# Moving the latent projection's weight splits and first units into the normalisation before it, and its rotary part to GpSimd

## The reference

```python
def _shared_latent(x, pos, wkv_a, kv_norm):
    kv = x @ wkv_a                      # 1024 -> 256 + 64
    ckv = _rms_norm(kv[..., :KV_LORA], kv_norm)
    kpe = _rope(kv[..., KV_LORA:], pos)
    return ckv, kpe
# and in _mla_query: _rms_norm(x @ wq_a, q_norm), 1024 -> 384
```

## Time and profile before

| | |
|---|---|
| median of three runs | 2543.57 us (2538.87 to 2545.26) |
| profiled execution | 2539.54 us, span 2537.5 us |
| TensorE busy | 2392.3 us, 94% of the span |
| VectorE / ScalarE / GpSimd busy | 51% / 30% / 13% |
| chain that ended last, by engine | PE 82%, DVE 10%, ACT 3%, issue 3%, DMA 1% |
| mean granted TensorE clock | 0.979 |

### The profile page before, as it was taken

How to read it: one execution, slowest core, us unless ns; L and a number is a source line. 1 busy time by engine, 2 the same in 40 slices (tenths; PEclk the granted TensorE clock), 3 DMA queues, 4 the chain that set the end, 5 groups by cost and what they waited for, 6 DMA issues and landing times.

```text
span 2537.5 us, 35304 instructions
## 1 busy us (share of the span) xinstructions
PE 2392.3 (94%) x14022; PEld 2178.8 (86%) x14022; DVE 1287.9 (51%) x2435; ACT 768.2 (30%) x1469; POOL 330.6 (13%) x300
## 2 busy tenths in 40 slices
PE   7899999999999968999998889799999999999997
PEld 7799999999999868898987677587998989999996
DVE  4733343333334675677767787635243443333336
ACT  2331111111111333555546566413311111111112
POOL 2400000000000410000006545033000000000006
PEclk9999999999999989999999999799999999999998
DMA  4121111111111031000005444321211110111111
GB/s 162 42 67 34 50 50 30 36 50 50 50 50 63 13 114 43 19 19 1 12 22 157 155 156 156 133 79 34 67 44 41 50 44 25 50 50 50 51 42 67
DMA packets 137073, 153.84 MB, mean 61 GB/s; under 512 B 10256, under 2 KB 114224, under 8 KB 136808
## 3 DMA queue, kind: packets, MB, share of 16 engines
q1 hardware_dynamic: 124656, 110.07, 13.9%
q0 software_dynamic: 12288, 41.95, 5.3%
HBM read 142.24 MB, written 10.32 MB: 60 GB/s over the span
## 4 chain that ended last, share of the span: by engine, by line
PE 82%; DVE 10%; ACT 3%; issue 3%; DMA 1%; POOL 0%; SPq 0%; ACTq 0%; DVEq 0%
PE ps L216 23%; PE ps L218 23%; PE ps L217 23%; DVE split L209 4%; PE ps L2136 2%; PE ps L2101 2%; ACT split L204 2%; PE ps L2116 1%; PE ps L2117 1%; PE ps L224 1%; PE ps L223 1%; PE ps L1646 1%; PE ps L2123 1%; DVE plain L292 1%; DVE plain L1889 1%
## 5 line engine op out<-in xcount | busy, mean ns | idle before, releaser
L216 PE MATMUL ps<-split 128*128 128x512 f32 (+6 forms) x3632 | 1236.8, 341 | 56.9 <-DVE split L209 31.9
L217 PE MATMUL ps<-split 128*128 128x512 f32 (+6 forms) x3632 | 1222.8, 337 | 0.0
L218 PE MATMUL ps<-split 128*128 128x512 f32 (+6 forms) x3632 | 1222.3, 337 | 0.0
L216 PEld LDWEIGHTS ps<-split 128*128 128x128 f32 x3632 | 689.6, 190 | 102.6 <-DVE split L209 37.0
L217 PEld LDWEIGHTS ps<-split 128*128 128x128 f32 x3632 | 689.8, 190 | 38.3 <-issue 1.5
L218 PEld LDWEIGHTS ps<-split 128*128 128x128 f32 x3632 | 689.9, 190 | 37.3
L204 ACT ACTIVATE split<-plain 128x1024 fp32r<-128x1024 f32 (+8 forms) x446 | 313.6, 738 | 594.8 <-PE ps L224 365.5
L209 DVE TENSOR_TENSOR split<-plain,split 128x1024 fp32r<-128x1024 f32 (+7 forms) x422 | 362.9, 884 | 190.3 <-ACT split L204 187.1
L998 DVE TENSOR_TENSOR plain<-plain,ps 128x350 f32<-128x350 f32 (+1 forms) x132 | 68.0, 515 | 552.9 <-ACT plain L952 552.3
L276 DVE TENSOR_TENSOR plain<-plain,ps 128x512 f32<-128x512 f32 x360 | 245.0, 685 | 197.0 <-PE ps L218 192.2
L209 DVE TENSOR_TENSOR split<-ps,split 128x512 fp32r<-128x512 f32 (+5 forms) x480 | 247.1, 554 | 136.6 <-ACT split L204 134.6
(11 more groups left out here) (147 smaller groups left out, 1432.1 us busy)
## 6 DMA issues: line engine op xcount, KB each, us to landing
plain<-w_gate SPq DMA_DIRECT2D x44, 512.0 KB, 4.6
plain<-w_up SPq DMA_DIRECT2D x44, 512.0 KB, 4.0
plain<-w_down SPq DMA_DIRECT2D x44, 512.0 KB, 4.4
plain<-x_prompt SPq DMA_DIRECT2D x8, 512.0 KB, 11.2
x_spill<-plain SPq DMA_DIRECT2D x1, 4096.0 KB, 13.9
plain<-wo SPq DMA_DIRECT2D x8, 512.0 KB, 5.3
plain<-x_spill SPq DMA_DIRECT2D x8, 512.0 KB, 7.2
y_prompt<-plain SPq DMA_DIRECT2D x8, 512.0 KB
```

Of the source, the lines that this page charges most:

```text
L216: pe.matmul(out, still[0], moving[0], start=start, stop=False)
L217: pe.matmul(out, still[0], moving[1], start=False, stop=False)
L218: return pe.matmul(out, still[1], moving[0], start=False, stop=stop)
```

## The change

Each block gets places of its own, so that blocks can be split at other times: block 0 in step 3 of the normalisation, 1, 2 and 3 in steps 5, 6 and 7, block 4 in step 11, blocks 5, 6 and the first half of 7 in the first three steps of the latent part, the second half of 7 (which overlies a kv block) when unit 8 is done. Each block is split in two instructions for its two chunks of 128 rows on either engine, and TensorE's units 0 and 9 wait chunk by chunk. Unit 0 moves before the transposes of tile 6, units 1 and 2 before those of tile 7, unit 3 before the tail's; the transposes of the latent rows stand behind unit u + 4 instead of u + 3. VectorE takes units 0 and 1 in step 11 (`behind`). The rotary part goes from VectorE to GpSimd with a semaphore of its own. ScalarE's squares go into PSUM bank 7, so it no longer waits for the output slot; VectorE's scale and GpSimd's rotary part wait for it instead. The diff, cut:

```diff
-def dve_norm_stage(dve, k, ph, nt, turn, scaled, unit0=0, extra=None):
+def dve_norm_stage(dve, k, ph, nt, turn, scaled, unit0=0, extra=None, behind=None):
     chain = Chain(dve, *k.s.at(ph + "_norm_steps", 0))
     for step in range(k.tiles + 5):
+        if behind is not None and step == k.tiles + 3:
+            behind(chain)
         if turn and 4 <= step:
             dve_turned_lo(dve, k, ph, step - 4, nt)
         if extra is not None:
...
         def between(step):
-            if step >= self.k.tiles + 2:
-                latent_unit(pe, self.k, step - self.k.tiles - 2)
+            for u in {1: (0,), 2: (1, 2), 3: (3,)}.get(step - self.k.tiles, ()):
+                latent_unit(pe, self.k, u)
...
-        if self.layer == 0 and step in (3, self.k.tiles + 1):
-            for n in ((0, 1) if step == 3 else (2, 3)):
+        if self.layer == 0:
+            for n in {3: (0,), 5: (1,), 6: (2,), 7: (3,), self.k.tiles + 3: (4,)}.get(step, ()):
                 latent_split(eng, self.k, n, act)
...
+        def takes(chain):
+            for u in range(2):
+                latent_take(dve, k, u, chain)
+
         def last():
             dve_norm_stage(dve, k, self.ph, nt, self.layer == 0, False, unit0=18 * (self.groups - 1),
-                           extra=lambda step: self.latent_weights(dve, step, False))
+                           extra=lambda step: self.latent_weights(dve, step, False),
+                           behind=takes if self.layer == 0 else None)
...
-            sp.wait_ge(s["lat_w_lo"], n - 3)
+            sp.wait_ge(s["lat_w_lo"], 2 * (n - 3))
...
         sp.wait_ge(s["lat_ready"], t + 1)
+        sp.wait_ge(s["lat_rope"], t + 1)
...
-def latent_split(eng, k, n, act):
+def latent_split(eng, k, n, act, chunks=(0, 1)):
...
     if act:
         if n == 0:
             eng.wait_ge(*s.at("ffn0_gu_done", 2 * PARTS * k.ffn[0].steps))
-        if n == 2:
+        if n == 1:
+            eng.wait_ge(*s.at("ffn0_unit_done", 18 * (k.ffn[0].groups - 1) + 10))
+        if n == 4:
             eng.wait_ge(*s.at("ffn0_unit_done", 18 * k.ffn[0].groups))
-        if n == 7:
-            eng.wait_ge(s["lat_unit_done"], k.tiles + 1)
         eng.wait_ge(s["lat_raw_in%d" % (n % 4)], 16 * (n // 4 + 1))
-        hi_part(eng, hi, k.lat_raw(n)).then_inc(s["lat_w_hi"], 1)
+        for c in chunks:
+            if (n, c) == (7, 1):
+                eng.wait_ge(s["lat_unit_done"], k.tiles + 1)
+            hi_part(eng, hi[c], k.lat_raw(n)[:, c, :]).then_inc(s["lat_w_hi"], 1)
     else:
-        eng.wait_ge(s["lat_w_hi"], n + 1)
-        lo_part(eng, lo, k.lat_raw(n), hi).then_inc(s["lat_w_lo"], 1)
+        for c in chunks:
+            eng.wait_ge(s["lat_w_hi"], 2 * n + c + 1)
+            lo_part(eng, lo[c], k.lat_raw(n)[:, c, :], hi[c]).then_inc(s["lat_w_lo"], 1)
...
 def latent_unit(pe, k, u):
     s, nt, half = k.s, k.ns + k.nm, k.tiles + 1
     t, w = u % half, latent_width(k, u)
-    if u == 0:
-        pe.wait_ge(*s.at("ffn0_unit_taken", 18 * k.ffn[0].groups))
-        pe.wait_ge(s["lat_w_lo"], 4)
-    if u == half:
-        pe.wait_ge(s["lat_w_lo"], 8)
+    if u < 3:
+        pe.wait_ge(*s.at("ffn0_unit_taken", 18 * k.ffn[0].groups - 2 + u))
     if u < half:
         pe.wait_ge(*s.at("ffn0_turned_lo", min(2 * t + 2, 2 * k.tiles + 1)))
     pe_unit_free(pe, k, "lat", u)
     bank = unit_bank(u)
     for kc in range(k.kc):
+        if t == 0:
+            pe.wait_ge(s["lat_w_lo"], 8 * (u // half) + kc + 1)
         hi, lo = k.lat_w(4 * (u // half) + kc // 2)
-        wt = (hi[:, kc % 2, :], lo[:, kc % 2, :])
+        wt = (hi[kc % 2], lo[kc % 2])
...
+        if u < half:
+            pe.wait_ge(s["lat_rope"], u + 1)
...
-    for step in range(2, latent_tasks(k) + 3):
+    for step in range(4, latent_tasks(k) + 4):
         if step < latent_tasks(k):
             latent_unit(pe, k, step)
-        if step >= 3:
-            turn(step - 3)
+        turn(step - 4)
...
-        if u == half:
-            latent_split(act, k, 7, True)
+        if u == half - 1:
+            latent_split(act, k, 7, True, (1,))
         if u < latent_tasks(k):
             n = P if u % half < k.tiles else nt
             rms = k.rank if u < half else k.q_w
             act.wait_ge(s["lat_unit_taken"], u + 1)
-            if u >= 3:
-                act.wait_ge(s["lat_turned"], u - 2)
-                if u - 3 < half:
-                    before = sum(4 if t == k.tiles else 2 for t in range(u - 2) if t % 3 == u % 3)
-                    act.wait_ge(s["lat_out%d" % (u % 3)], 16 * before)
-            act.activation(k.lat_row[0:n, u % 3, 0:rms], k.lat_in[0:n, u % 2, 0:rms], ACT.Square,
+            if u == 0:
+                act.wait_ge(*s.at("ffn0_turned_lo", 2 * k.tiles + 1))
+            act.activation(k.ps[0:n, 7, 0:rms], k.lat_in[0:n, u % 2, 0:rms], ACT.Square,
                            accum_out=k.lat_ss[0:n, u:u + 1]).then_inc(s["lat_square"], 1)
             act.wait_ge(s["lat_square"], u + 1)
             act.activation(k.lat_root[0:n, u:u + 1], k.lat_ss[0:n, u:u + 1], ACT.Sqrt, bias=k.rms_eps[0:n, 0:1],
                            scale=1.0 / rms).then_inc(s["lat_root"], 1)
-            if u in (3, 5, 7):
-                latent_split(act, k, 4 + (u - 3) // 2, True)
+            if u < 3:
+                latent_split(act, k, 5 + u, True, (0, 1) if u < 2 else (0,))
...
+def row_slot_free(eng, k, u):
+
+    if u >= 3:
+        eng.wait_ge(k.s["lat_turned"], u - 2)
+        if u - 3 <= k.tiles:
+            before = sum(4 if t == k.tiles else 2 for t in range(u - 2) if t % 3 == u % 3)
+            eng.wait_ge(k.s["lat_out%d" % (u % 3)], 16 * before)
+
+
+def latent_take(dve, k, u, chain):
+    s, nt, half = k.s, k.ns + k.nm, k.tiles + 1
+    t, w = u % half, latent_width(k, u)
+    dve.wait_ge(s["lat_unit_done"], u + 1)
+    ps = k.ps[:, unit_bank(u), 0:w]
+    if u >= 2:
+        dve.wait_ge(s["lat_ready"], u - 1)
+        if u - 2 < half:
+            dve.wait_ge(s["lat_rope"], u - 1)
+    if t < k.tiles:
+        dve.tensor_copy(k.lat_in[:, u % 2, 0:w], ps).then_inc(s["lat_unit_taken"], 1)
+    else:
+        chain.link(dve.tensor_copy(k.lat_in[0:nt, u % 2, 0:w], ps[LO:LO + nt]))
+        dve.tensor_tensor(k.lat_in[0:nt, u % 2, 0:w], k.lat_in[0:nt, u % 2, 0:w], ps[0:nt], ALU.add)\
+           .then_inc(s["lat_unit_taken"], 1)
+
...
+        row_slot_free(dve, k, u)
         chain.link(dve.tensor_scalar(k.lat_var[0:n, col], k.lat_ss[0:n, col], 1.0 / rms, RMS_EPS, ALU.mult, ALU.add))
         newton_rsqrt(dve, k.lat_scale[0:n, col], k.lat_root[0:n, col], k.lat_var[0:n, col], k.lat_newton[0:n, col], chain)
-        ins = dve.scalar_tensor_tensor(out=out[:, 0:rms], in0=x[:, 0:rms], scalar=k.lat_scale[0:n, col],
-                                       in1=gain[0:n, 0:rms], op0=ALU.mult, op1=ALU.mult)
-        if u >= half:
-            ins.then_inc(s["lat_ready"], 1)
-            return
-
-        r, h = k.rank, k.rope // 2
-        table = k.rope_rows[0:n, t, :]
-        ins = dve.tensor_tensor(out[:, r:r + 2 * h], x[:, r:r + 2 * h], table[:, 0:2 * h], ALU.mult)
-        dve.tensor_tensor(k.rope_tmp[0:n, 0:h], x[:, r + h:r + 2 * h], table[:, 2 * h:3 * h], ALU.mult)
-        chain.link(dve.tensor_tensor(k.rope_tmp[0:n, h:2 * h], x[:, r:r + h], table[:, 3 * h:4 * h], ALU.mult))
-        chain.link(dve.tensor_tensor(out[:, r:r + 2 * h], out[:, r:r + 2 * h], k.rope_tmp[0:n, 0:2 * h], ALU.add))
-        dve.tensor_copy(out[:, r + 2 * h:r + 4 * h], out[:, r:r + 2 * h]).then_inc(s["lat_ready"], 1)
+        dve.scalar_tensor_tensor(out=out[:, 0:rms], in0=x[:, 0:rms], scalar=k.lat_scale[0:n, col],
+                                 in1=gain[0:n, 0:rms], op0=ALU.mult, op1=ALU.mult).then_inc(s["lat_ready"], 1)
 
...
-    for step in range(latent_tasks(k) + 4):
-        if step == half:
-            latent_split(dve, k, 7, False)
-        if step < latent_tasks(k):
-            take(step)
-            if step in (3, 5, 7):
-                latent_split(dve, k, 4 + (step - 3) // 2, False)
-        if 1 <= step <= latent_tasks(k):
+    for step in range(1, latent_tasks(k) + 4):
+        if 2 <= step < latent_tasks(k):
+            latent_take(dve, k, step, chain)
+        if step == half - 1:
+            latent_split(dve, k, 7, False, (1,))
+        if step <= latent_tasks(k):
             finish(step - 1)
+        if step <= 3:
+            latent_split(dve, k, 4 + step, False, (0, 1) if step < 3 else (0,))
         if step >= 4:
             lo(step - 4)
...
+    s, r, h = k.s, k.rank, k.rope // 2
+    chain = Chain(pool, s["lat_rope_steps"])
+    pool.wait_ge(s["lat_tables_in"], 48)
+    for u in range(k.tiles + 1):
+        n = P if u < k.tiles else k.ns + k.nm
+        x, out, table = k.lat_in[0:n, u % 2, :], k.lat_row[0:n, u % 3, :], k.rope_rows[0:n, u, :]
+        pool.wait_ge(s["lat_unit_taken"], u + 1)
+        row_slot_free(pool, k, u)
+        pool.tensor_tensor(out[:, r:r + 2 * h], x[:, r:r + 2 * h], table[:, 0:2 * h], ALU.mult)
```

(32 more changed lines are left out.)

## The result

The changed kernel takes 2528.93 us (median of five runs, 2522.49 to 2531.07), the kernel before 2541.63 on the same chip (five runs, 2538.87 to 2545.26): a ratio of 0.994, 95% interval 0.9926 to 0.9953, a gain of 12.7 us. The profiled execution took 2531.07 us with a span of 2529.3.

A forecast was written before the change was run, and what follows sets the result against it. TensorE, busy 94% of the span, was taken as the bound; its waits and low clock between 853 and 1000 us were the target. Front part -1.4 plus latent part 14.8 gave 13.4 us faster, median near 2530.5, range 2515 to 2541.

The forecast's parts named there:

- The hold on VectorE: VectorE instructions with both inputs in SBUF wait, each, until the running GpSimd instruction ends; met at steps 3, 5, 6, 7.
- R1: Rival: the second chunk slips in before GpSimd's addition; each loop 2.4 us shorter, median 2521; chance 0.18.
- R2: Rival: no hold, the long subtractions were slow for another cause; 320-element ones run in 0.4 us, median 2512; chance 0.05.
- The loops: Steps with held splits, normalisation to normalisation: 10.8 us each, before 6.2; tile 6's normalisation 13 us late.
- TensorE's waits: Down projection: TensorE stands about 1.6 us in step 6, 3.7 in step 7, 3.8 in the tail step.
- The front part's end: Units 0 to 3 and transposes of tiles 5 to 8 done at 918.8, before 917.45: 1.4 us later.
- the low clock: Lower granted TensorE clock after waits; counted in the front part as 1.5 us in the last down unit.
- The latent part: From the kv units through the q units: the 10.4 us wait and its low clock go, net gain about 14.8 us.
- The wait before unit 5: Latent part: squares of unit 0 wait for the tail's low parts, so TensorE stands about 1.0 us.
- Sum: Front part -1.4 plus latent part 14.8: 13.4 us faster, taken as 13.
- The rotary part on GpSimd: Five instructions, about 1.6 us a unit, costing TensorE nothing; VectorE was no bound, earlier rows remove most of 2.3 us.
- The spill: Issued near 912, lands 13.9 us later near 927; finishing unit 3 near 930 leaves it hidden by a microsecond.

The follow-up runs named there:

- late_window: Changed kernel with ScalarE's high parts of blocks 0 to 3 between root and normalisation, VectorE's low parts right behind the scale; 2511.77 us, ratio 0.9884.
- short_gpsimd: Changed kernel with GpSimd's gain and bias in layer 0's last normalisation on only 8 of 1024 columns, the rest left out; 2512.94 us, ratio 0.9887.
- whole_blocks: Changed kernel with blocks 0 to 3 split in one instruction of 640 elements each instead of two of 320; 2519.06 us, ratio 0.9911.
- rotary_long: Changed kernel with GpSimd's second rotary instruction repeated twelve times more in each unit; 2549.81 us, ratio 1.0031.
- rotary_vector: Changed kernel with the five rotary instructions of each unit back on VectorE, behind the scale; 2535.99 us, ratio 0.9981.
- squares_slot: Changed kernel with ScalarE's squares written into the row's output slot again, ScalarE waiting for that slot; 2528.95 us, ratio 0.9947.
- rotary_double: Changed kernel with GpSimd's second rotary instruction repeated four times more in each unit; 2532.78 us, ratio 0.9956.

## Why the prediction was right, step by step

Its total was within a third of a microsecond (13 us forecast, 12.7 measured). That close is luck: the interval of the ratio is 3.4 us wide to either side, and the parts err in both directions. The median is 2528.93 for 2530.5 because the kernel before took 2541.63 beside it and not 2543.57. The mechanism held, but for one term in the front part.

- **The hold on VectorE** was read rightly from four instructions of the earlier trace rows. All eight chunks were held; no second one slipped in (R1), and R2 needs chunks of 0.4 us; where nothing holds them, the time is R2's 2512 (late_window 2511.77, short_gpsimd 2512.94). The Trainium skill's "GPSIMD Engine Reference" (Key points) names contention with VectorE instructions that have two SBUF inputs, and the runs here agree (2.42 to 2.66 us for 320 elements beside GpSimd, 0.48 without). The Trainium skill's "Advanced Engine Details and Errata" (Mode Summary) speaks of the 2-port modes alone; for this case it is too narrow.
- **The loops**: 10.63 us for 10.8. The normalisation of tile 6 starts at 900.13 - 1.36 = 898.8 for 899.4.
- **TensorE's waits**: 2.1, 3.3 and 3.3 for 1.6, 3.7 and 3.8. (The one of 1.8, in step 3, is the 2.4 of before.)
- **The front part's end** was the step that failed: 921.72 - 1.36 = 920.4, not 918.8, so the part loses 2.9 us and not 1.4. The term that was mis-sized is the low clock. The forecast had it once, 1.5 us in the last down unit. The trace has it three times. After the 3.3 us wait of step 7, seven matmuls of 512 columns are 0.42 us apart for 0.23 (1.3 us); this costs nothing, as TensorE then stands until the next additions. The second stretch comes after the next wait, in the last down unit, and takes only 0.8 there. That unit runs from 895.4 to 898.2 on the forecast's clock, for 895.9 to 899.4 (the forecast's own 888.6 + 6.8 is 895.4), which hides 1.2 of the miss. From its end to unit 4 pass 22.2 us, for 17.9 + 1.5 = 19.4: the waits are 2.0 for 1.5, the transposes of tile 5 still run at the low clock (0.6), and the third stretch begins at 907.99: twelve matmuls of 320 columns are 0.267 apart for 0.147, 1.4 us. This last one was not in the sum. It stands behind a 1.3 us wait for GpSimd, eight transposes and a 0.5 us wait, but that order alone does not bring it. In whole_blocks the same order (1.44 and 0.54) is followed by matmuls 0.147 apart. So it is in rotary_long, whose program is the same up to here: its low clock came earlier, behind the wait of 2.09 us, and its front part took 66.1 us from the start of the stretch, for 67.6. What decides this stays open. The timeline of TensorE in the changed kernel, then in rotary_long:

```profile
907.55 0.78 PE L401 MATMUL ps<-plain 128*128 128x128 f32 x4 [0.54 <-DVE split L209]
...
908.40 0.47 PE L217 MATMUL ps<-split 128*128 128x320 f32 x1
```

```profile
875.28 0.56 PE L216 MATMUL ps<-split 128*128 128x512 f32 x1 [2.09 <-DVE plain L276]
...
876.07 0.63 PE L218 MATMUL ps<-split 128*128 128x512 f32 x1
...
907.33 0.66 PE L401 MATMUL ps<-plain 128*128 128x128 f32 x4 [0.57 <-DVE split L209]
...
907.98 0.31 PE L217 MATMUL ps<-split 128*128 128x320 f32 x1
```

- **The latent part** came out as forecast. From unit 4's start to the last turns pass 980.04 - 921.72 = 58.3 us (57.3 + 1.0 + 0.3 = 58.6), where the earlier trace rows have 73.5: 15.2 gained for 14.8. The wait before unit 5 is 0.84 for 1.0, and the tail from there to the heads 8.47 for 8.4.
- **Sum**: -2.9 + 15.2 = 12.3, which is the 146.7 - 134.4 of the stretch.
- **The rotary part on GpSimd** costs what was estimated: 0.32 us for 64 columns, 0.25 for 32, some 1.45 us a unit for 1.6. The statement that VectorE was no bound, and that the move only removes waits of 2.3 us, was too weak. Without it, the split that unit 9 waits for comes 4.5 us later, and a third of the latent part's gain is lost (rotary_vector). The forecast reached the right sum since it took all edits together and asked only when block 7 is split.
- **The spill** was not hidden by a microsecond. "The tail step has no split" overlooked the other VectorE instructions with two SBUF inputs there, gain and bias of the tail. The multiplication by the gain, at 910.65, met GpSimd's addition for tile 7 (910.59 to 912.97) and took 3.40 us, where it took 1.21 before. SP waits for the addition of the tail's bias behind it (done at 915.3) and not only for tile 7's rows, the spill is issued at 916.71 and lands at 931.2, and finishing unit 3 waited 0.7 us and GpSimd 4.5. TensorE's list shows none of it.

What each edit is worth, from the kernels that undo it: the rotary part 5.4 us of the stretch, the units' places 2.7, the squares 0.5. In the changed kernel, rotary_vector, squares_slot and rotary_double the front part took 67.55 to 67.57 us, so differences of this size can be read off one profile each, except where the clock falls in another place, as in rotary_long. The weights' places were not undone alone. Their part is the rest and is argued: splits of blocks 5 to 7 in the first three steps end the 10.4 us wait, while those of steps 5 to 7 pay the hold.

## What to carry to other kernels

When VectorE instructions with both inputs in SBUF are put into a pipeline where GpSimd works, count the holds and not the elements: each pays the rest of the running GpSimd instruction, and everything behind it in VectorE's queue, up to TensorE's banks, is late by as much. Look for the gap in which GpSimd waits for its input and put them there; here that turned a gain of 12.7 us into one of about 30. An engine whose work a unit is shorter than TensorE's can still be the bound when it starts behind: divide its backlog by the difference of the paces, and see what is due before that.

## What the runs showed of the hardware

- The hold lasts to the end of the running GpSimd instruction, after which the VectorE instruction still takes about its own time: 320 and 640 elements both took 2.42 us, 320 alone 0.48. It also met a 24-partition instruction (3.40 us for 1.21). Instructions with one input in PSUM were not held (0.68 us beside a running GpSimd instruction).
- GpSimd's short instructions are lengthened too: its 64-column multiplication at 941.22, beside VectorE's scale at 941.07, took 0.52 us for 0.32, and its copy at 942.62 took 0.99 for 0.24, ending 0.1 after VectorE's split (942.98 to 943.52). Alone that copy would have ended before the split began; VectorE then ran an addition with one input in PSUM (942.57), and what held the copy up to the split is not shown. The timeline of GpSimd in the changed kernel, the same copy of two units:

```profile
939.95 0.24 POOL L1306 COPY plain<-plain 128x64 f32<-128x64 f32 x1
...
942.62 0.99 POOL L1306 COPY plain<-plain 128x64 f32<-128x64 f32 x1
```

- In the changed kernel the granted clock fell behind waits of 3.3 us between dense matmuls (0.70 and 0.64 over the next 3.2 us) and not behind those of 1.75 and 2.1 us, after which matmuls of 512 columns were 0.23 us apart from the second on. The length of the wait does not decide it alone: in rotary_long the same wait of 2.09 us was followed by 0.54 over the next 3.2 us (matmuls 0.43 apart), and in the kernel before one of 2.44 us by seven slow matmuls, while whole_blocks has none behind 1.91.
